# Attention and Hyena joined: keys transposed once and doubled by a copy, queries turned inside attention, an even transform ahead of the last short convolution

## The reference, cut to what matters

```python
q = rms_norm(q.reshape(B, L, N_HEADS, HEAD_DIM), p['q_gain'][l])
k = rms_norm(k.reshape(B, L, N_KV_HEADS, HEAD_DIM), p['k_gain'][l])
if latent:
    q = rope_2d(q)
    k_all = jnp.concatenate([rope_2d(k), ctx_k.astype(k.dtype)], axis=1)
    v_all = jnp.concatenate([v, ctx_v.astype(v.dtype)], axis=1)
s = jnp.einsum('bqkgd,bskd->bkgqs', q_blk, k, preferred_element_type=jnp.float32) * scale
p = jax.nn.softmax(s, axis=-1).astype(v.dtype)
...
uc = up[:, :-2] * short_w[0] + up[:, 1:-1] * short_w[1] + up[:, 2:] * short_w[2] + short_b
z = parts[0]
for o in range(HY_ORDER):
    zc = jnp.fft.irfft(jnp.fft.rfft(z, n=2 * L, axis=1) * spec[None, :, o], n=2 * L, axis=1)[:, :L]
    z = parts[o + 1] * (zc + z * skip[o].astype(jnp.float32))
```

## Time and profile before

| | us |
|---|---|
| median of 3 runs | 1669.75 (1667.23 to 1669.85) |
| the profiled execution | 1671.05 |
| its span | 1669.2 |
| busy: TensorE | 1502.6 (90%) |
| busy: TensorE weight loads | 1085.1 (65%) |
| busy: VectorE | 943.8 (57%) |
| busy: ScalarE | 370.5 (22%) |
| busy: GpSimd | 367.9 (22%) |

### The profile page before, as it was taken

One profiled execution on the slowest core, in us unless ns is written; L12 is line 12 of the kernel. 1 busy time (PEld: TensorE's weight loads), 2 busy tenths in 40 slices (PEclk: granted clock), 3 DMA queues, 4 the chain that ended last, 5 costly groups with the idle time before them and its releaser, 6 DMA issues. The chain is left out here.

```text
span 1669.2 us, 22612 instructions
## 1 busy us (share of the span) xinstructions
PE 1502.6 (90%) x8510; PEld 1085.1 (65%) x8510; DVE 943.8 (57%) x1557; ACT 370.5 (22%) x710; POOL 367.9 (22%) x623
## 2 busy tenths in 40 slices
PE   6689988999997899938999997999489999999985
PEld 3357667544443688837888884555378888888852
DVE  3768877356653999985666652534633333333316
ACT  2552341111111111115665551000000000000004
POOL 0330330011110000000131227655322222122114
PEclk9799999999998899969999996999689999999998
DMA  9412123233322122230000004111448999998845
GB/s 293 167 61 94 32 86 107 76 102 106 127 97 85 57 66 66 73 111 1 1 2 2 2 1 152 63 64 51 176 175 321 330 333 330 329 330 328 307 172 220
DMA packets 102742, 229.25 MB, mean 137 GB/s; under 512 B 12807, under 2 KB 70759, under 8 KB 93896
## 3 DMA queue, kind: packets, MB, share of 16 engines
q1 hardware_dynamic: 78968, 195.86, 33.0%
q0 software_dynamic: 10736, 19.77, 3.4%
q10 hardware_dynamic: 12960, 12.59, 2.2%
HBM read 204.66 MB, written 38.98 MB: 146 GB/s over the span
## 5 line engine op out<-in xcount | busy, mean ns | idle before, releaser
L1102 PE MATMUL PS<-buffer 128*128 128x128 f32 (+7 forms) x5638 | 1258.8, 381 | 90.1 <-DVE buffer L1587 26.7
L1102 PEld LDWEIGHTS PS<-buffer 128*128 128x128 f32 (+2 forms) x5638 | 872.7, 196 | 447.9 <-issue 312.9
L1587 DVE TENSOR_TENSOR buffer<-buffer 128x256 f32<-128x256 f32 (+15 forms) x452 | 260.0, 596 | 19.7 <-ACT buffer L853 5.6
L1105 PE MATMUL PS<-buffer 128*128 128x128 f32 x1176 | 166.5, 284 | 41.5 <-DVE buffer L1587 25.0
L1105 PEld LDWEIGHTS PS<-buffer 128*128 128x128 f32 x1176 | 137.5, 155 | 70.6 <-issue 49.2
L1587 DVE TENSOR_TENSOR buffer<-PS,buffer 128x512 f32<-128x512 f32 (+3 forms) x143 | 93.9, 683 | 137.0 <-PE PS L1102 116.2
L1587 DVE TENSOR_TENSOR buffer<-buffer,PS 128x256 f32<-128x256 f32 (+3 forms) x55 | 27.5, 500 | 205.9 <-PE PS L1102 195.3
L2007 DVE TENSOR_SCALAR_CACHE_REDUCE buffer<-PS 128x1152 f32<-128x1152 f32 (+1 forms) x72 | 89.2, 1239 | 41.5 <-PE PS L1102 40.5
L996 ACT ACTIVATE buffer<-buffer 128x1152 f32<-128x1152 f32 (+1 forms) x72 | 83.7, 1163 | 103.8 <-DVE buffer L2007 103.8
L1072 ACT ACTIVATE buffer<-PS 128x256 f32<-128x256 f32 x33 | 12.7, 384 | 367.1 <-PE PS L1102 367.1
L2023 DVE COPY buffer<-PS 128x640 f32<-128x640 f32 x64 | 52.8, 824 | 60.5 <-PE PS L1105 60.5
(11 more groups left out here) (166 smaller groups left out, 941.0 us busy)
## 6 DMA issues: line engine op xcount, KB each, us to landing
buffer<-in_exp_w_gate SPq DMA_DIRECT2D x33, 1024.0 KB, 7.0
buffer<-in_exp_w_up SPq DMA_DIRECT2D x33, 1024.0 KB, 9.5
buffer<-in_exp_w_down SPq DMA_DIRECT2D x33, 1024.0 KB, 9.3
buffer<-in_w_mod SPq DMA_DIRECT2D x24, 1024.0 KB, 5.9
filter_spectra<-buffer ACTq DMA_DIRECT2D x88, 128.0 KB, 1.7
buffer<-filter_spectra SPq DMA_DIRECT2D x44, 256.0 KB, 2.6
buffer<-in_w_in SPq DMA_DIRECT2D x9, 1024.0 KB, 5.2
buffer<-expert_outputs SPq DMA_DIRECT2D x4, 1536.0 KB, 17.0
```

Of the source, the lines that this page charges most:

```text
L1102: return nc.tensor.matmul(out, lhsT, rhs, start=start, stop=stop)
L1105: return nc.tensor.transpose(out, in_, ident)
L1587: return dve.tensor_tensor(out, a, b, op)
```

## The change

- **Turn.** Keys are split in their natural rows, all ten tiles in one go for each key head (`split_keys`). They are transposed as 128x64 blocks, which give 64 partitions, four blocks of ten tiles (two key heads, high and low). ScalarE copies a block of 1280 columns to partitions 0 to 63 of `kT`, and VectorE copies it from there to partitions 64 to 127 (`double_keys`). Only the queries of tile 0 are turned here.
- **Attention.** The queries of tile t+1 are split by VectorE at the first head of tile t, behind its probability copy, turned two heads at a time by TensorE at the heads 2 to 5, ahead of the probability transposes, into free columns of bank 5, and copied out by VectorE behind its probability copy.
- **Hyena.** `hy_even` of the first half is put ahead of the last feature's short convolution, behind the wait for the last projection and for the tokens of the feature before. TensorE's first three forward products come ahead of the last feature's transposes.
- **Cache.** The cached keys and values take the place of the decay rows, and their loads move to before the load of the inverse transform matrices.

```diff
@@ places
+        HEADS_AT = {8 * t + i: (t + 1, 2 * i - 4) for t in range(NTILE - 1) for i in (2, 3, 4, 5)}
+        KEY_BLOCKS = [(v, s) for v in range(KV) for s in range(2)]
@@ SyncE
             for r in range(3):
                 sp.wait_ge(rs["spec"][r], SPEC_STORED[r])
+            sp.wait_ge(sem("window_ready"), PASSES * NTILE)
+            load(cache_k, I["cache_k"], "cache_loaded")
+            load(cache_v, I["cache_v"], "cache_loaded")
...
             sp.wait_ge(sem("hyena_done"), 1)
-            load(cache_k, I["cache_k"], "cache_loaded")
-            load(cache_v, I["cache_v"], "cache_loaded")
@@ ScalarE
-            for s in range(10):
...
+            for n, (v, s) in enumerate(KEY_BLOCKS):
+                act.wait_ge(sem("rows_turned"), n + 1 + (n > 1))
+                act.copy(kT[0:HD, s, v, :], PS[0:HD, 1536 * (n % 2):1536 * (n % 2) + 10 * P]).then_inc(sem("rows_copied"), 1)
+                if n == 1:
+                    act.wait_ge(sem("rows_turned"), 3)
+                    act.copy(qT[:, :, 0:P], PS[:, 3072:4096].rearrange("p (h t) -> p h t", h=HEADS)).then_inc(sem("rows_copied"), 1)
@@ TensorE
-            for i in range(3):
-                to_tokens(FEATS - 1, i)
...
-            pe.wait_ge(sem("tokens_copied"), 3 * FEATS)
             for q in range(3):
                 forward(q)
+            for i in range(3):
+                to_tokens(FEATS - 1, i)
             for q in range(4 * HY_CLS):
                 if q + 3 < 4 * HY_CLS:
                     forward(q + 3)
+                if q == 2:
+                    pe.wait_ge(sem("tokens_copied"), 3 * FEATS)
                 inverse(q)
...
+            def turn_keys(n):
+                v, s = KEY_BLOCKS[n]
+                pe.wait_ge(sem("rows_split"), n + 1 + (n > 1))
+                if n >= 2:
+                    pe.wait_ge(sem("rows_copied"), n - 1)
+                for t in range(NTILE + 1):
+                    key = {NLAT: 9, NTILE: 8}.get(t, t)
+                    at = 1536 * (n % 2) + P * key
+                    last = turn(PS[0:HD, at:at + P], k_split[:, s, t, HD * v:HD * (v + 1)].bitcast(F32))
+                last.then_inc(sem("rows_turned"), 1)
...
+            turn_keys(0)
+            turn_keys(1)
+            pe.wait_ge(sem("rows_split"), 3)
+            for h in range(HEADS):
+                last = turn_head(PS[:, 3072 + P * h:3072 + P * (h + 1)], h)
+            last.then_inc(sem("rows_turned"), 1)
+            turn_keys(2)
+            turn_keys(3)
+
+            def turn_heads(i):
+                t, h0 = HEADS_AT[i]
+                pe.wait_ge(sem("rows_split"), 5 + t)
+                for h in (h0, h0 + 1):
+                    last = turn_head(bank(5, P, at=P * (1 + h - h0)), h)
+                if h0 + 2 == HEADS:
+                    last.then_inc(sem("rows_turned"), 1)
...
             def turn_probs(i):
                 n = NTILE if ATT[i][1] < NLAT else 1
+                if i:
+                    pe.wait_ge(sem("probsT_d"), i)
+                if i - 1 in HEADS_AT:
+                    pe.wait_ge(sem("scores_side_copied"), 4 * HEADS_AT[i - 1][0] + HEADS_AT[i - 1][1] // 2 + 1)
+                if i in HEADS_AT:
+                    turn_heads(i)
                 pe.wait_ge(sem("exp_ready"), i + 1)
@@ VectorE, features
+                if f + 1 == FEATS:
+                    dve.wait_ge(sem("tokens_copied"), 3 * f)
+                    hy_even(HY_PHASES[0][1])
...
-            dve.wait_ge(sem("tokens_copied"), 3 * FEATS)
             halves = [c for o, c in HY_PHASES]
 
-            hy_even(halves[0])
             hy_odd(halves[0])
             hy_odd_tiles(halves[0])
+            dve.wait_ge(sem("tokens_copied"), 3 * FEATS)
@@ VectorE, turn
+            def split_keys(v):
...
+                next_but_one(dve.tensor_copy(high[:, 0:NTILE, :], rows))
+                own(dve.tensor_copy(high[:, NTILE, :], cache_k[:, d]))
+                dve.sem_inc(sem("rows_split"), 1)
+                next_but_one(tt(low[:, 0:NTILE, :], rows, high[:, 0:NTILE, :].bitcast(F32), ALU.subtract))
+                tt(low[:, NTILE, :], cache_k[:, d], high[:, NTILE, :].bitcast(F32), ALU.subtract).then_inc(sem("rows_split"), 1)
...
+            def double_keys(n):
+                v, s = KEY_BLOCKS[n]
+                dve.wait_ge(sem("rows_copied"), n + 1 + (n > 1))
+                dve.tensor_copy(kT[HD:P, s, v, :], kT[0:HD, s, v, :].bitcast(F32)).then_inc(sem("scores_side_copied"), 1)
+
+            split_keys(0)
+            high_heads(0)
+            low_heads(0)
+            split_keys(1)
+            for n in range(len(KEY_BLOCKS)):
+                double_keys(n)
@@ VectorE, attention, behind the probability copy of i
+                if i in HEADS_AT:
+                    t, h = HEADS_AT[i]
+                    dve.tensor_copy(qT[:, h:h + 2, P * t:P * (t + 1)],
+                                    bank(5, 2 * P, at=P).rearrange("p (h t) -> p h t", h=2)).then_inc(sem("scores_side_copied"), 1)
+                h, t = ATT[i]
+                if t + 1 < NTILE and h == 0:
+                    dve.wait_ge(sem("rows_turned"), 5 + t if t else 3)
+                    high_heads(t + 1)
+                    low_heads(t + 1)
```

More of the change, by code:

```diff
@@ L283, in build @@
         kT = low.take(4 * 10 * P, "p (s v t) -> p s v t", s=2, v=KV)
-        q_split = low.take(2 * 2 * HEADS * HD, "p (r h s d) -> p r h s d", r=2, h=HEADS, s=2)
-        k_split = low.take(2 * 2 * KV * 2 * HD, "p (r s v c d) -> p r s v c d", r=2, s=2, v=KV, c=2)
+        k_split = low.take(2 * (NTILE + 1) * KV * HD, "p (s t n) -> p s t n", s=2, t=NTILE + 1)
+        low = Columns(nc, TOP0 - 2 * HEADS * HD, TOP0, F32R)
+        q_split = low.take(2 * HEADS * HD, "p (h s d) -> p h s d", h=HEADS, s=2)
         low = Columns(nc, MATS0 + HEADS * T + 4 * 10 * P, TOP0)
@@ L294, in build @@
         w_out = gates.take(KT * D, "p (k n) -> p k n", k=KT)
-        cache_k = gates.take(P)
-        cache_v = gates.take(P)
+        cache_k, cache_v = decay[:, 0:P], decay[:, P:2 * P]
         nmax = gates.take(72)
@@ L1347, in _, with turn_head @@
                     forward(q + 3)
+                if q == 2:
+                    pe.wait_ge(sem("tokens_copied"), 3 * FEATS)
                 inverse(q)
             pe.wait_ge(sem("hyena_done"), 1)
[L1352 to L1364, removed]
+            def turn_keys(n):
[8 more added lines that the diff above has]
+                last.then_inc(sem("rows_turned"), 1)
+            def turn_head(out, h):
+                return turn(out, q_split[:, h, :, :].rearrange("p s d -> p (s d)").bitcast(F32))
+            turn_keys(0)
[13 more added lines that the diff above has]
+                    last.then_inc(sem("rows_turned"), 1)
             def scores(i):
@@ L1371, in scores @@
                     pe.wait_ge(sem("max_ready"), i)
+                if t and h == 0:
+                    pe.wait_ge(sem("scores_side_copied"), 4 * t + 4)
                 for s in range(2):
@@ L1381, in turn_probs @@
                     pe.wait_ge(sem("probsT_a"), i)
-                    pe.wait_ge(sem("probsT_d"), i)
                 for k in range(n):
@@ L1423, in spread_scales @@
                 last.then_inc(sem("scales_spread"), 1)
-            pe.wait_ge(sem("qk_copied"), 10)
+            pe.wait_ge(sem("rows_copied"), len(KEY_BLOCKS) + 1)
+            pe.wait_ge(sem("scores_side_copied"), len(KEY_BLOCKS))
             scores(0)
@@ L1983, in _ @@
             dve.sem_inc(sem("hyena_done"), 1)
-            dve.wait_ge(sem("cache_loaded"), 32)
[L1987 to L1999, removed]
+            def split_keys(v):
+                d = slice(HD * v, HD * (v + 1))
+                rows = qkv[:, :, HEADS * HD + HD * v:HEADS * HD + HD * (v + 1)]
+                high, low = k_split[:, 0, :, d], k_split[:, 1, :, d]
+                next_but_one(dve.tensor_copy(high[:, 0:NTILE, :], rows))
[3 more added lines that the diff above has]
+                tt(low[:, NTILE, :], cache_k[:, d], high[:, NTILE, :].bitcast(F32), ALU.subtract).then_inc(sem("rows_split"), 1)
@@ new lines, in high_heads, with low_heads @@
+            def high_heads(t):
+                q = qkv[:, t, 0:HEADS * HD].rearrange(heads, h=HEADS)
+                own(dve.tensor_copy(q_split[:, :, 0, :], q))
+            def low_heads(t):
+                q = qkv[:, t, 0:HEADS * HD].rearrange(heads, h=HEADS)
+                tt(q_split[:, :, 1, :], q, q_split[:, :, 0, :].bitcast(F32), ALU.subtract).then_inc(sem("rows_split"), 1)
+            dve.wait_ge(sem("cache_loaded"), 32)
+            def double_keys(n):
+                v, s = KEY_BLOCKS[n]
+                dve.wait_ge(sem("rows_copied"), n + 1 + (n > 1))
+                dve.tensor_copy(kT[HD:P, s, v, :], kT[0:HD, s, v, :].bitcast(F32)).then_inc(sem("scores_side_copied"), 1)
```

## The result

The changed kernel takes 1656.62 us in the median of 4 runs (1655.8 to 1660.6), the kernel before 1669.8. The ratio is 0.9929 with a 95% interval of 0.9912 to 0.9945: 11.9 us or 0.7% faster. A second timing of the same kernel gave 0.9940 (0.9918 to 0.9962), 10 us.

What follows compares the result with a forecast made beforehand. No engine bounded the whole: it priced the convolution's start, the turn's ring and attention's full TensorE with its even-head chain. -4.1 - 15.5 + 4.7 + 5.0 = -9.9 us from 1671.05 gave 1661.2, as median 1660.0; range 1655.5 to 1667.

Steps and rivals of the forecast that it cites:

- The convolution's start: Start of the Hyena convolution: even transform ahead of the last short convolution brings the first weighing 4.1 us earlier.
- Rival 3: Convolution's start: early transform buys nothing, as spectra or a lower clock hold the first weighings; 1664.1 us, chance 0.08.
- The turn: Turn of queries and keys before attention: scores start at 744.7 instead of 760.49; 15.5 us gain taken.
- the cast's line: Turn: the doubling copy priced by VectorE's cast times at two widths, 0.83 us at 1280 columns.
- Rival 1: Turn: clock stays at half throughout, scores start 3.3 us later; 1663.3 us, chance 0.07.
- The added transposes: Attention: 64 query transposes on full TensorE cost 6.8 us, less 2.1 filling its waits; 4.7 us added.
- The splits: Attention, first head of each tile: VectorE's cast and subtraction delay an even maximum by 0.72 us; seven tiles 5.0.
- Tile 0: Attention's first tile: the splits have 1.05 us of room there and cost nothing.
- Rival 2: Attention: none of the added work is absorbed, transposes 6.8 and splits 9.2 us; 1666.2 us, chance 0.12.
- rival 4: Attention: VectorE paces it, every operation before a maximum delays it fully, costing 29.4 us; 1679.6 us, chance 0.05.
- The sum: Whole kernel: the four terms together, -9.9 us on the profiled execution.

Runs made afterwards that it cites:

- experiment 2: Changed kernel with the early even transform and first forward products put back behind the last tokens; ratio to the kernel before 0.9956.
- experiment 3: Kernel before with only the earlier loads of cached keys and values, their buffers in the decay rows' place; ratio to the kernel before 0.9986.
- experiment 5: Changed kernel without turning queries inside attention, all tiles scoring from tile 0's queries; 1650.89 us, ratio to the kernel before 0.9903.
- experiment 4: Changed kernel with the query splits behind the second head's probability copy instead of the first's; ratio to the kernel before 0.9906.
- experiment 6: Changed kernel with query splits behind the second head and turned heads at iterations 3, 5, 7 and 9; ratio to the kernel before 0.9904.

## Why the prediction was right

- *The convolution's start*, -4.1: right, -4.2. It starts at 529.21 as worked out, and 547.85 was forecast for 547.78. What was missed is the clock: the forward products put ahead brought it to 1.00 for the last transposes, so the spectra had 1.2 us more room than worked out. Rival 3, that the spectra or the clock eat it, is out by the weighing that waited for nothing and by experiment 2.
- *The turn*, -15.5: right, 10.55 us behind the gate where 10.3 followed from the steps. Two terms were a little off and cancelled in part. The clock rose later, and ScalarE was faster than in proportion, 1.22 us a block for 1.27. The doubling copy took 0.82 for the 0.83 of the cast's line: writing other partitions than it reads cost nothing. The sum is right; how much of it is the move of the queries stays open (experiment 3).
- *Rival 1, the half clock through the turn*: out. The granted clock rose from 0.50 to 1.00 (1.2 to 2.4 GHz) while nothing but transposes had run. Busy time of the changed kernel by stretch:

```profile
734.00:735.00 1.00, 1.00 (x6) 0.83 (x5) 0.84 (x3) 0.76 (x1) 0.00 (x0) 0.50 0.98 377
735.00:736.00 1.00, 1.00 (x11) 0.99 (x9) 0.62 (x1) 0.56 (x1) 0.00 (x0) 0.99 0.98 393
```

  It came after 3.8 us of transposes instead of the 3 of the earlier trace rows. The Trainium skill says in TensorE: Matmul & The Clock Gate, Part 4: PE-mode transpose, that the full clock doesn't engage for transposes; that rule doesn't hold here.
- *The added transposes*, +4.7: right, 4.1 to 4.9 by experiment 5 and 4.7 by the pairs of heads. A pair is 0.30 us longer, not 0.43, since an odd iteration's transposes fill a wait (7.16 us forecast as 7.15).
- *The splits*, +5.0: right in place and size. They cost 4.4 by experiment 5, 4.7 to 5.5 by experiment 4 and 4.8 by the seven pairs. Tile 0 wasn't quite free: there the scores behind the delayed maximum stood 0.59 us in the changed kernel, 0.47 in the kernel before and not at all with the splits later. In the tile shown the two value matmuls are 781.88 - 774.33 = 7.55 us apart, with 774.33 the start of the twenty before, 0.69 more than 6.86, where 0.72 were forecast. Rival 2, full payment, would have made it 1.15 and is out; so is rival 4, with attention 9.3 us longer and not 29.4.
- *The sum*: -9.9 forecast, -10.5 in the profiled pair, -11.9 and -10.0 by the two ratios. The terms were right and each was seen in its own stage. That the median came out 3.4 us below the forecast is not in them: the starts of executions differ more than I allowed for, and one single run, of 1654.6, lies below the range. Nor was the upper end added up from all bounds: it took 5.0 for the splits, whose own bound was 9.2, and with 4.2 more it would have been 1666.6 + 4.2 = 1670.8, not 1667. The range was narrower at that end than the working behind it, and the result didn't test this.

## What to carry to other kernels

Where engines pass work along in a ring, price a change by the chain that has no slack, and look which parity or position it has: the same two VectorE operations cost 5 us behind head 0 and nothing that the profile shows behind head 1, with 0.3 us of room beside both. That other even heads are like head 0 follows from the chain and wasn't run. When a stage gets shorter, ask how much of it was only moved. The turn lost 13.8 us by its new order, but by the estimate in experiment 3 some 7 of these are queries that moved into attention, where they cost 9.3. Only with splits and turned heads at better places (experiment 6: attention 249.6 us, 2.5 more than before) does the move clearly pay, by the same estimate. The untested rival is a turn of wide blocks that keeps all queries. And look beside the headline of a change for what pays: here the copy in the name is a loss of 0.6 us.

## What the runs showed of the hardware

- Transposes alone brought TensorE from the half clock to the full one, after about 3 us in the kernel before, 3.8 in the changed one and 6 in that of experiment 3. In the other seven profiles it was 3.1 to 4.3.
- The same first instructions of attention ran at 0.50 in the kernel before and at 1.00 in that of experiment 3, with the same idle time of 1.59 us ahead of the first score, and that was worth some 2 us. What decides it stays open, also whether it is the kernel or the single execution.
- A VectorE copy of 1280 columns from partitions 0 to 63 to partitions 64 to 127 took 0.82 us. A copy of 1280 columns out of PSUM took ScalarE 1.22 us for 64 partitions and 1.23 for 128.
- Much of the spread between executions is there within the first 60 us. The first modulation by ScalarE, ahead of which all these kernels have the same instructions, starts at 60.61 in the changed kernel and at 56.77 in that of experiment 6, whose span is the shortest, 1643.6. By the first weighing (547.78 and 541.59) the 3.8 us have become 6.2.

```profile
60.61 1.50 ACT L895 ACTIVATE buffer<-buffer 128x512 f32<-128x512 f32 x2
```

```profile
56.77 1.50 ACT L895 ACTIVATE buffer<-buffer 128x512 f32<-128x512 f32 x2
```

  Its cause was not looked for; the stage lengths don't carry it, which is why the experiments were read by them.
